# A ninth weight buffer for the two expert mixtures, laid partly in rooms that stood beside others

## The reference, cut to what matters

```python
N_EXPERTS = 16; TOP_K = 2; D_MODEL = 1024; D_FF_EXPERT = 512
def moe(h, router_w, router_b, w1, w3, w2):
    scores = jax.nn.sigmoid((h @ router_w).astype(jnp.float32))
    ...                                   # best group, then the top 2 experts inside it
    comb = (jax.nn.one_hot(e_idx, N_EXPERTS) * w[..., None]).sum(axis=1)
    y = jnp.zeros_like(h)
    for e in range(N_EXPERTS):
        y = y + comb[:, e:e + 1] * ((jax.nn.silu(h @ w1[e]) * (h @ w3[e])) @ w2[e])
    return y
```

## Time and profile before

| | |
|---|---|
| median of 3 runs | 2481.53 us (2480.44 to 2483.8) |
| profiled execution: its time | 2480.0 us |
| profiled execution: its span | 2478.2 us |
| TensorE busy | 2346.6 us, 95% |
| VectorE, ScalarE, GpSimd busy | 1150.7, 496.6, 545.1 us |
| read from HBM | 489.63 MB |
| first mixture, from its first expert product to its last | 484.2 to 765.7 us |
| second mixture, the same | 979.6 to 1226.4 us |

### The profile page before, as it was taken

How to read it: one execution, slowest core, us unless ns; L and a number is a source line. 1 busy time by engine, 2 the same in 40 slices (tenths; PEclk the granted TensorE clock), 3 DMA queues, 4 the chain that set the end, 5 groups by cost and what they waited for, 6 DMA issues and landing times.

```text
span 2478.2 us, 35301 instructions
## 1 busy us (share of the span) xinstructions
PE 2346.6 (95%) x13820; PEld 1665.6 (67%) x13820; DVE 1150.7 (46%) x2655; ACT 496.6 (20%) x1111; POOL 545.1 (22%) x364
## 2 busy tenths in 40 slices
PE   6999989899984998999799999999999999999999
PEld 3455544533432456333478888999997888899996
DVE  1346441401003354132246887645544688764553
ACT  2233331211113321211111122022210112212220
POOL 0000000000001001000040004737934000563793
PEclk9999999999997998999899999999999999999999
DMA  9403289789997335999755434455444443444543
GB/s 279 142 35 119 84 311 333 253 302 358 380 384 266 88 133 198 346 373 382 290 175 160 136 136 157 149 170 170 163 162 145 153 141 136 144 164 143 171 162 111
DMA packets 293269, 502.02 MB, mean 203 GB/s; under 512 B 22896, under 2 KB 115312, under 8 KB 293104
## 3 DMA queue, kind: packets, MB, share of 16 engines
q1 hardware_dynamic: 282336, 474.39, 55.2%
q0 software_dynamic: 4096, 14.16, 1.8%
q10 hardware_dynamic: 6672, 11.21, 1.2%
HBM read 489.63 MB, written 10.09 MB: 202 GB/s over the span
## 4 chain that ended last, share of the span: by engine, by line
PE 87%; DVE 3%; DMA 3%; SPq 3%; DVEq 1%; issue 1%; ACT 1%; PEld 0%; ACTq 0%; PEldq 0%; POOL 0%; POOLq 0%
PE bank L3216 21%; PE bank L3240 16%; PE bank L3235 5%; PE bank L705 4%; PE bank L1167 3%; PE bank L2022 3%; PE bank L2034 3%; PE bank L2453 2%; PE bank L2603 2%; PE bank L739 2%; PE bank L290 2%; PE bank L1198 2%; SPq L584 1%; SPq L1046 1%; PE bank L2661 1%; DMA spare<-in_exp_w 1%
## 5 line engine op out<-in xcount | busy, mean ns | idle before, releaser
L3216 PE MATMUL bank<-hT,ring 128*128 128x256 f32 x2048 | 452.9, 380 | 0.0
L3216 PEld LDWEIGHTS bank<-hT,ring 128*128 128x128 f32 x2048 | 384.5, 190 | 52.6 <-issue 2.7
L3730 DVE SCALAR_TENSOR_TENSOR y_conf<-y_glu,s_cw,y_conf 128x256 f32<-128x256 f32 x480 | 195.0, 479 | 0.8
L4100 POOL TENSOR_TENSOR y_sacc<-y_cx,s_sw 128x512 f32<-128x512 f32 x24 | 32.7, 1363 | 469.2 <-DVE y_conf L3730 466.1
L1489 POOL IOTA r_prio<- 128x16 f32 x2 | 0.3, 151 | 579.9 <-DVEq L138 579.9
L3240 PE MATMUL bank<-hT,ring 128*128 128x128 f32 x1056 | 125.4, 275 | 0.0
L3240 PEld LDWEIGHTS bank<-hT,ring 128*128 128x128 f32 x1056 | 121.8, 192 | 0.1
L884 DVE TENSOR_TENSOR hidA<-sgT,bank 128x256 f32<-128x256 f32 x16 | 6.7, 422 | 197.5 <-ACT sgT L837 85.8
L2022 PE MATMUL bank<-ring,hT 128*128 128x384 f32 (+1 forms) x224 | 88.9, 540 | 0.7 <-DMA ring<-in_even_w_in 0.7
L2034 PE MATMUL bank<-ring,hT 128*128 128x384 f32 (+1 forms) x224 | 88.8, 539 | 0.0
L3240 PE MATMUL bank<-hT,y_qkv 128*128 128x128 f32 x736 | 85.8, 275 | 0.0
(11 more groups left out here) (717 smaller groups left out, 4274.2 us busy)
## 6 DMA issues: line engine op xcount, KB each, us to landing
extra<-in_exp_w SPq DMA_DIRECT2D x72, 1024.0 KB, 13.0
ring<-in_exp_w SPq DMA_DIRECT2D x72, 1024.0 KB, 14.0
ring<-in_ada_w SPq DMA_DIRECT2D x24, 2048.0 KB, 9.7
ring<-in_w_in SPq DMA_DIRECT2D x24, 2048.0 KB, 7.7
ring<-in_w_up SPq DMA_DIRECT2D x44, 1024.0 KB, 7.1
ring<-in_w_in SPq DMA_DIRECT2D x32, 1024.0 KB, 7.8
spare<-in_exp_w SPq DMA_DIRECT2D x24, 1024.0 KB, 12.9
h_tok<-in_exp_w SPq DMA_DIRECT2D x18, 1024.0 KB, 13.0
```

The costliest lines, as they stand in the source:

```text
L3216: mm = pe.matmul(b, w[:, k, j * P:(j + 1) * P], moving(k), start=(k == 0), stop=(k == KT - 1))
L3730: ins = dve.scalar_tensor_tensor(conf[:, f, :], src, cw[:, f, k:k + 1], conf[:, f, :], ALU.mult, ALU.add)
```

## The change

Both mixtures get a buffer more, so `N_BUF` is 9. In `moe` its first half lies in the rows of `gateb` that held the mixer's gate (used for the last time in the stage before), its second in a new tile `ninth` of half the size. In `moe_summed` it is a new tile of full size, and the product with the gate, which had a tile `gated` of its own, is laid in the first gate's rows there. Room for the new tiles comes from laying `picks`, `whose`, `lane_picks` and two scratch tiles of `route` (`part`, `fuller`) in `ye`, whose results come later. The initial loads are now nine; since the ninth in the old order would be that of expert 3, which is not known yet, `order` places down 2 ahead of the two loads of expert 3. The ninth buffer is loaded right behind `spare`, with no wait of its own; the buffer in `h_tok` is now the ninth in line, for load 8.

```diff
@@ moe
-            whose = sb(mem, f"whose{l}", [P, N_EXP, N_EXP])
             buffers.append(two(sb(mem, f"spare{l}", [P, KT * COLS])))
+            buffers.append([gateb[:, 0, :, :].rearrange("p c d -> p (c d)"), sb(mem, f"ninth{l}", [P, KT // 2 * COLS])])
 
             buffers.append(two(h_tok[:, :, :].rearrange("p m d -> p (m d)")))
             order = [("up", 0, 0), ("up", 0, 1)]
             for e in range(1, N_EXP):
-                order += [("up", e, 0), ("up", e, 1), ("down", e - 1, 0)]
+                ups, down = [("up", e, 0), ("up", e, 1)], [("down", e - 1, 0)]
+                order += down + ups if e == FIXED else ups + down
                 for j in range(N_BUF):
-                    if j == N_BUF - 2:
+                    if j == N_BUF - 3:
                         sp.wait_ge(stage_done.sem, entered)
                     elif j == N_BUF - 1:
                         sp.wait_ge(h_stored, 16 * nt)
-                    elif j >= len(extra):
+                    elif len(extra) <= j < len(extra) + RING:
                         used, value = used_at[n0 + j - len(extra) - RING]
                         sp.wait_ge(used.sem, value)
                     load_weights(sp, j, slice(order[j][1], order[j][1] + 1))
-            route(l, mem, h_rows, h_stored, h_tok, rank, wgt, mine, placed, place_of, tables, iota, passes, nt, widths)
-            picks = sb(mem, f"picks{l}", [P, 2 * nt, P])
+            ye = sb(mem, f"ye{l}", [P, 2, 2 * COLS])
+            whose = ye[:, 1, 768:1024].rearrange("p (a b) -> p a b", b=N_EXP)
+            route(l, mem, ye[:, 1, 0:n_tok], ye[:, 1, 512:768], h_rows, h_stored, h_tok, rank, wgt, mine, placed, place_of, tables, iota, passes, nt, widths)
+            picks = ye[:, 0, :].rearrange("p (i s) -> p i s", s=P)
                         if which_was == "up":
-                            sp.wait_ge(up_done, p * 32 + (2 * e_was + half_was + 4 - 32 * back))
+                            sp.wait_ge(up_done, p * 32 + max(2 * e_was + half_was + 4 - 32 * back, 0))
@@ moe_summed (the same edits to order, to the waits and to route's call)
             buffers.append(two(sb(mem, f"spare{l}", [P, KT * COLS])))
+            buffers.append(two(sb(mem, f"ninth{l}", [P, KT * COLS])))
+            ye = sb(mem, f"ye{l}", [P, N_YE, D])
+            picks = ye[:, 1, 512:1024].rearrange("p (i s) -> p i s", s=P)
-            lane_picks = sb(mem, f"lane_picks{l}", [P, 3, 2 * nt, P])
+            lane_picks = ye[:, 0:2, :].rearrange("p a d -> p (a d)")[:, 0:12 * P].rearrange("p (b i s) -> p b i s", b=3, s=P)
-            gated = sb(mem, f"gated{l}", [P, 2, COLS])
+            gated = gateb[:, 0, 0, :].rearrange("p (a n) -> p a n", a=2)
@@ route
-        part = sb(mem, f"r_part{l}", [P, n_tok])
-        fuller = sb(mem, f"r_fuller{l}", [P, N_EXP, N_EXP])
+        fuller = fuller_room.rearrange("p (a b) -> p a b", b=N_EXP)
```

More of the change, by code:

```diff
@@ L610, in moe @@
             hidB = sb(mem, f"hidB{l}", [P, 4 * SA])
-            ye = sb(mem, f"ye{l}", [P, 2, 2 * COLS])
             picks_ready, idx_made, idx_ready = sem("picks_ready"), sem("idx_made"), sem("idx_ready")
@@ L657, in freed @@
                         if which_was == "up":
-                            sp.wait_ge(up_done, p * 32 + (2 * e_was + half_was + 4 - 32 * back))
+                            sp.wait_ge(up_done, p * 32 + max(2 * e_was + half_was + 4 - 32 * back, 0))
                         else:
-                            sp.wait_ge(down_done, p * parts[N_EXP] + (parts[e_was + 1] + 4 - parts[N_EXP] * back))
+                            sp.wait_ge(down_done, p * parts[N_EXP] + max(parts[e_was + 1] + 4 - parts[N_EXP] * back, 0))
                     with sp.If_ne(sp.to_reg(p), 0):
@@ L1060, in _ @@
                     load_weights(sp, j, slice(order[j][1], order[j][1] + 1))
-            route(l, mem, h_rows, h_stored, h_tok, rank, wgt, mine, placed, place_of, tables, iota, passes, nt, widths)
-            picks = sb(mem, f"picks{l}", [P, 2 * nt, P])
+            ye = sb(mem, f"ye{l}", [P, N_YE, D])
+            route(l, mem, ye[:, 2, 0:n_tok], ye[:, 2, 512:768], h_rows, h_stored, h_tok, rank, wgt, mine, placed, place_of, tables, iota, passes, nt, widths)
+            picks = ye[:, 1, 512:1024].rearrange("p (i s) -> p i s", s=P)
             idx = sb(mem, f"idx{l}", [P, N_EXP], mybir.dt.int32)
@@ L1072, in moe_summed @@
             hidB = sb(mem, f"hidB{l}", [P, 4 * SA])
-            ye = sb(mem, f"ye{l}", [P, N_YE, D])
             lane = sb(mem, f"lane{l}", [P, 3, P])
-            lane_picks = sb(mem, f"lane_picks{l}", [P, 3, 2 * nt, P])
+            lane_picks = ye[:, 0:2, :].rearrange("p a d -> p (a d)")[:, 0:12 * P].rearrange("p (b i s) -> p b i s", b=3, s=P)
             both = sb(mem, f"both{l}", [P, 2 * nt, 2, N_EXP])
@@ L1455, in build, with route @@
     MAX_PASSES = 8
-    def route(l, mem, h_rows, h_stored, h_tok, rank, wgt, mine, placed, place_of, tables, iota, passes, nt, widths):
+    def route(l, mem, part, fuller_room, h_rows, h_stored, h_tok, rank, wgt, mine, placed, place_of, tables, iota, passes, nt, widths):
         f0, a0, b0 = bank_full.n, act_out.n, bank_free_act.n
@@ L1542, in _ @@
             act.wait_ge(bank_full.sem, f0 + LOGITS)
-            act.activation(part[:, :], bank[0][:, 0:n_tok], ACT.Copy).then_inc(act_out.sem, 1)
+            act.activation(part, bank[0][:, 0:n_tok], ACT.Copy).then_inc(act_out.sem, 1)
             act.wait_ge(bank_full.sem, f0 + TURNED)
```

## The result

The change makes the kernel slower: 2492.16 us median of 7 runs (2488.36 to 2498.78) against 2482.89 us of before (7 runs, 2480.44 to 2485.16). The ratio is 1.0040, 95% interval 1.0030 to 1.0049, that is 7 to 12 us more. I had forecast 2471 us, with 2467 to 2477 as the range, and given 0.05 to slower.

A forecast was written before the change was run, and what follows sets the result against it. Both mixtures' ends were taken to hang on weight loads, DMA engines idle early for want of buffers and full later. 2480.0 - 10.9 + 0.5 = 2469.6 us, given as a median of 2471.0, range 2467 to 2477.

The forecast's parts named there:

- slower: Rival: stores and ninth load hinder each other at mixture starts, `h_stored` comes far later; 2487 us, chance 0.05.
- The order of down 2 and expert 3: Loads of both mixtures: expert 3 refills the buffers of loads 0 and 1 either way; the new order costs nothing.
- release k now admits the load that release k+1 admitted before: Mixture loops: each buffer release admits a load one release earlier, so the last landing comes one load earlier.
- Both signs of being wrong: First expert product moving by over 2 us, or the full stretch of DMA engines not ending one load earlier.
- A load more in the idle stretch: Mixture starts: a ninth load fills idle DMA time, leaving one load fewer later; 5.52 and 5.42 us, sum -10.9 us.
- The start: Mixture starts: ninth load delays `h_stored` by one load and load 8 may delay the first gather; +0.5 us.
- The tail's clock: Last products of both mixtures: lower TensorE clock after idling may change; taken as 0, with -3.4 and +1.7 in the range.
- The rooms: Tiles laid in others' space: no wait added, instruction shapes kept, so no cost.
- Rival B: One mixture loses its gain at the start because the gather comes late, some 5 us; 2476 us, chance 0.07.
- C, a wait for code: Experts' start: code loading waits behind load 8; 2476.5 us for one mixture, chance 0.04, or 2481.5 for both, chance 0.03.

The follow-up runs named there:

- e3: Changed kernel, same nine buffers and load order, but each load takes its buffer in order of release, in both mixtures: 2475.86 us, ratio 0.9967 to before.
- e2: Kernel before, eight buffers, only down 2 placed ahead of expert 3's two loads in both mixtures: 2504.32 us, ratio 1.0079 to before.
- e8: Changed kernel with load 8 issued after the first two gathers landed, and the old order of loads: 2470.80 us, ratio 0.9957 to before.
- e4: e3 with load 8 issued only when the first two gathers have landed, in both mixtures: 2470.61 us, ratio 0.9944 to before.
- e1: Changed kernel without the ninth buffers and the new order, only the shared rooms kept: 2483.29 us, ratio 0.9999 to before.
- e6: Changed kernel with buffers taken by release in the first mixture alone: 2483.04 us, ratio 1.0008 to before.
- e7: Kernel before, eight buffers, down 2 placed between expert 3's two loads, one place early, in both mixtures: 2491.99 us, ratio 1.0042 to before.
- e5: Changed kernel with only load 8 moved behind the first two gathers, in both mixtures: 2488.30 us, ratio 1.0035 to before.

## Why the prediction was wrong

**The step that failed** is the one headed "The order of down 2 and expert 3", where I wrote "TensorE uses down 2 behind up 3 as before. Nothing." The first sentence is true, and it is the reason why the second is false. The order of loads and the order of uses had been one and the same; the buffer of load j is that of load j - N_BUF only as long as they are. With down 2 two places early, its buffer is released two places late, and SP stands with load 17. The runs put 16.3 us on it with nine buffers (changed kernel to e3, medians) and 21.4 us with eight (e2). Forecast: 0.

The same mistake sits in "release k now admits the load that release k+1 admitted before". That holds for loads 11 to 16 (9 and 10 keep their releases), and I had followed only loads 9 to 11 in the order of SP's queue. The place where it breaks is load 17, eight loads behind the first in the loop. Both signs of being wrong that I had named came: the first expert product of the first mixture moved by 2.1 us (484.21 to 486.31), and the full stretch ended later and not one load earlier.

**A load more in the idle stretch** was right in mechanism and size. I forecast -10.9 us for both mixtures. e8, which has the ninth load and neither the swap nor the start's cost, gives 0.9957 (-14 to -7 us), and e4 0.9944 (-17 to -11). By mixture e8 is 5.9 and 8.4 us under before, 7.0 and 6.2 under e1; the forecast was 5.5 and 5.4.

**The start** was right in mechanism in the first mixture, and too small. `h_stored` slipped by 6.8 us and not 5.5, and the turn of rows by 2.0 us and not 0.5; the later `h_stored` accounts for 1.3 of this 1.5. In the second mixture I had `h_stored` 5.4 us late behind the ninth load, and it slipped by 0.1 us (in e3 and e6 by 1.3 and 1.7): that step was wrong too, and did no harm. The forecast was +0.5 us for both. Measured: 5.3 us from e3 to e4 by the medians and 3 us by the traces, though that also counts what e4 gains over before: in e3 TensorE began the first turn of rows 29.4 us after the load into `spare` was issued, in before 28.0, in e4 28.1. To this comes the clock in the first product, 0.50 in e3 and 1.00 in e4, 6.54 us for 3.65 in these two executions. The counters had room, whatever one takes (no run shows it): SP was done with load 8's issues at 474.97 us, and POOL's gather went out at 477.47 for 477.44.

**The tail's clock.** I had looked for the clock at the tail only, and had put the slow products there down to the idle time before them. Before, the clock was 0.51 from 761 to 764 us behind a wait of 2.35 us, and 0.50 from 1219 to 1221 us behind one of 2.04 us. In the changed kernel TensorE waited 2.35 and 2.03 us there, the clock was 1.00, and the same products took 3.65 and 1.93 us for 5.35 and 3.62:

```profile
1229.64 1.93 PE L1208 MATMUL bank<-extra,hidB 128*32 128x256 f32 x32 [2.03 <-DMA extra<-in_exp_w]
```

So both products gained the 1.7 us that I had left open, in this one execution, and the wait before them did not settle their clock.

**The rooms** cost nothing, as forecast (e1).

**The rivals.** None was the right one. The time came out slower, but not by the mechanism of "slower" (0.05). That was given to `h_stored` slipping by 13.5 us in the first mixture and 15.2 in the second; it slipped by 6.8 and 0.1. Rival B's loss at the start was there in part. C, a wait for code, was not looked for by itself; as the stall and the start account for the loss, nothing is left for it.

**The sum after the fact**, medians: ninth load and late load 8 -12.3 us, load 8 back before the gathers +5.3, stall in both mixtures +16.3: +9.3, which is what the changed kernel measured. These are differences between the kernels' medians, so the sum closes by itself; what other runs add is that the stall (e2, e6, e7) and the ninth load (e8) show where they are tried alone. The start tried alone (e5) is not clear of noise.

## What to carry to other kernels

When loads are issued in order into a ring of buffers, write the order of uses beside the order of loads and follow a moved load through its buffer's next turn: here the cost of a load that came two places early stood N_BUF loads later, as a stall of the issuing queue (21.5 us at load 17), and not where it was moved. Two ways out did equally well here, once load 8 stood behind the gathers: buffers taken in the order of their release (e4, 2470.61 us), and loads left in the order of their uses (e8, 2470.80 us). And a stall can leave TensorE busy, as here for all of 560 to 580 us, and be paid all the same: the DMA engines were full (share 1.04) from 580 to 760 us, and it cost 9 to 12 us in the first mixture.

Look for a load that is not needed for long and stands in front of a small transfer that everybody waits for. Here moving it behind the gathers was worth 5 us by the medians without the stall (e3 to e4), and 3 us with it (e5), which alone is not clear of noise.

## What the runs showed of the hardware that I had not expected

The first expert product took from 3.65 to 6.54 us for the same 16 matmuls, by the clock that TensorE was granted (1.00, or 0.50 for a stretch of it). In e4, e5 and e8 it was 1.00 throughout and the product took 3.65 or 3.66 us. In before it was 0.50 from 485 to 488 us: 5.35 us. In e3 it was 0.50 from 485 to 491 us and in the changed kernel too: 6.54 and 6.20 us. These last two had waited longest for the rows, 2.92 and 3.53 us for 1.52 to 1.66 in before, e1, e4, e5, e7 and e8.

The wait does not settle it alone. With the start of before, e1 and e7 have 5.35 us and e2 3.65; e2 had its stretch at 0.50 from 479 to 482 us, ahead of the rows. And e6, with the start of e3, has 5.35 us: its clock was 0.50 from 478 to 481 us and again from 489 to 491. So where the stretch at 0.50 fell changed between these profiles, and up to 2.9 us of a first product with it. A difference of this size between two profiles is no proof of a cause here.
